# Throw-away matrix products on TensorE at a dozen of its waits in a two-block transformer kernel

## The reference, cut to what matters

```python
# first block, layer l
h = x * (1 + scale1) + shift1
y = token_mixer(h, ...)                       # attention branch + gated branch, then w_out
x = layer_norm(ALPHA * x + gate1 * y, ...)
y = moe_ffn(x * (1 + scale2) + shift2, ...)   # router, 64 experts, shared expert
x = layer_norm(ALPHA * x + gate2 * y, ...)
# second block
y, yc = attention_mixer(h, hc, ...)           # then MLP on x and on the context
y, _  = rwkv_mixer(h, hc, ...)                # wkv_scan forward and backward, group norm, read-out
x = x + gt2 * sq_relu_mlp(rmsnorm(x) * (1 + sc2) + sh2, w1, w2)
```

## Time and profile before

| | |
|---|---|
| median of 3 runs | 3715.33 us (3712.76 to 3722.76) |
| profiled execution, its own time | 3722.76 us |
| its span | 3722.7 us |
| TensorE busy | 3370.9 us, 91% |
| mean granted TensorE clock over the span | 0.956 |

### The profile page before, as it was taken

The page is one execution under the profiler, slowest core; times in us unless marked ns, Lnnn a source line. Parts: engine busy times, 40 slices in busy tenths (PEclk is TensorE's granted clock), DMA queues, the critical chain, the costliest instruction groups (busy, mean ns, idle before and its releaser), DMA issues.

```text
span 3722.7 us, 68873 instructions
## 1 busy us (share of the span) xinstructions
PE 3370.9 (91%) x29944; PEld 2469.4 (66%) x29944; DVE 1214.7 (33%) x2371; ACT 650.1 (17%) x1258; POOL 215.4 (6%) x186
## 2 busy tenths in 40 slices
PE   7998899999888889999979999999998889887899
PEld 5776466666667556656657664448877777786788
DVE  1344132233334323323345452010324454444200
ACT  0111011111110111111123231000023313332100
POOL 0000000000000000000000000000004410341000
PEclk9998999999899899999989999999999999998999
DMA  7655398899474469969912351224431013100342
GB/s 275 221 216 224 152 386 331 349 402 385 161 273 154 181 245 372 402 274 382 392 67 81 137 191 68 79 78 149 147 141 48 4 34 125 37 4 3 128 155 102
DMA packets 116171, 703.07 MB, mean 189 GB/s; under 512 B 11296, under 2 KB 11472, under 8 KB 49760
## 3 DMA queue, kind: packets, MB, share of 16 engines
q1 hardware_dynamic: 112224, 685.47, 47.5%
q0 software_dynamic: 3584, 12.25, 1.0%
HBM read 696.62 MB, written 1.05 MB: 187 GB/s over the span
## 4 chain that ended last, share of the span: by engine, by line
PE 41%; DVE 5%; ACT 2%; issue 1%; POOL 1%; DVEq 0%; ACTq 0%; POOLq 0%; PEldq 0%
PE ps L1518 9%; PE ps L1505 9%; PE ps L2148 7%; PE ps L204 4%; PE ps L1855 4%; DVE arena L137 2%; ACT arena L120 1%; PE ps L544 1%; PE ps L571 1%; PE ps L342 1%; PE ps L2530 1%; PE ps L2160 1%; PE ps L2153 1%; DVE arena L141 1%; PE ps L559 1%
## 5 line engine op out<-in xcount | busy, mean ns | idle before, releaser
L204 PE MATMUL ps<-arena 128*128 128x256 f32 (+2 forms) x2432 | 637.8, 425 | 45.6 <-issue 17.1
L204 PEld LDWEIGHTS ps<-arena 128*128 128x128 f32 (+1 forms) x2432 | 475.8, 197 | 201.6 <-issue 124.6
L120 ACT ACTIVATE arena<-ps 128x512 f32<-128x512 f32 (+1 forms) x526 | 265.2, 504 | 1632.6 <-PE ps L204 384.9
L1098 PE MATMUL ps<-arena 128*64 128x256 f32 x4096 | 484.9, 387 | 33.1 <-issue 32.9
L1098 PEld LDWEIGHTS ps<-arena 128*64 128x64 f32 x4096 | 320.3, 140 | 198.1 <-issue 91.6
L2148 PE MATMUL ps<-arena 64*64 64x64 f32 x10496 | 310.4, 226 | 53.6 <-issue 19.5
L1505 PE MATMUL ps<-arena 128*128 128x512 f32 (+1 forms) x1024 | 334.1, 489 | 10.3 <-DVE arena L146 10.3
L2148 PEld LDWEIGHTS ps<-arena 64*64 64x64 f32 x10496 | 296.9, 141 | 67.7 <-issue 34.5
L1518 PE MATMUL ps<-arena 128*128 128x256 f32 x1536 | 332.0, 379 | 0.0
L1518 PEld LDWEIGHTS ps<-arena 128*128 128x128 f32 x1536 | 291.8, 190 | 40.1 <-issue 0.5
L137 DVE TENSOR_TENSOR arena<-arena,ps 128x512 f32<-128x512 f32 (+1 forms) x276 | 163.1, 591 | 461.1 <-PE ps L2148 237.9
(11 more groups left out here) (190 smaller groups left out, 2557.8 us busy)
## 6 DMA issues: line engine op xcount, KB each, us to landing
arena<-in_w_gate SPq DMA_DIRECT2D x128, 1024.0 KB, 8.5
arena<-in_w_up SPq DMA_DIRECT2D x128, 1024.0 KB, 11.7
arena<-in_w_down SPq DMA_DIRECT2D x128, 1024.0 KB, 8.9
arena<-in_mlp SPq DMA_DIRECT2D x80, 1024.0 KB, 4.7
arena<-in_w_ada SPq DMA_DIRECT2D x48, 1024.0 KB, 7.2
arena<-in_ada SPq DMA_DIRECT2D x48, 1024.0 KB, 4.8
arena<-in_w_in SPq DMA_DIRECT2D x30, 1024.0 KB, 5.6
arena<-in_w_rkv SPq DMA_DIRECT2D x20, 1024.0 KB, 4.8
```

Of the source, the lines that this page charges most:

```text
L120: self.e.activation(out, in_, func, bias=bias, scale=scale, **more).then_inc(*self.done(key))
L204: ins = pe.matmul(out, a, b, start=start and i == 0, stop=stop and i == len(pairs) - 1)
L1098: ins = pe.matmul(psum.of["gu", l, new][64 * ab:64 * ab + 64, i_ * 256:i_ * 256 + 256], xe[:, k, new % 2 * 128 + 64 * ab:new % 2 * 128 + 6 ...
```

## The change

A helper `keep_warm(pe, b, n)` issues n fp32 products of the identity with 256 columns of `condr` into a bank that has been taken and freed; the real products overwrite the result. It is called at nine places of the source.

```diff
+        def keep_warm(pe, b, n):
+            for _ in range(n):
+                pe.matmul(b[:, 0:256], ident[:, :], condr[:, 0:256], start=True, stop=True)
@@ turned_pe, after the four banks are freed, before reach(ready(0))
+            keep_warm(pe, psum.of["turned", l, which, 0], (7 if which else 22) if l or which else 0)
@@ mixer_pe
-            reach(pe, *at["gated", l])
             for a in range(2):
                 b, old = psum.take(("obT", l, a), ("obT out", l, a))
                 freed(pe, old)
+                if a == 0:
+                    keep_warm(pe, b, 4)
+                    reach(pe, *at["gated", l])
@@ gather
                 freed(pe, old)
+                if Q == k == 0:
+                    keep_warm(pe, b, 7)
                 reach(pe, *at["chosen", l, Q])
@@ mlp_pe
+                    if i == c == 0:
+                        keep_warm(pe, b, (12, 6)[l])
@@ turning_pe(pe, s, src, warm=0)
+                if k2 == 0 and warm:
+                    keep_warm(pe, b, warm)
+                    reach(pe, *at["ln", ("moe", 1), 1])
@@ attention_pe
-            reach(pe, *at["ln", ("moe", 1), 1])
-            turning_pe(pe, 0, XS[:, :])
+            turning_pe(pe, 0, XS[:, :], 10)
@@ scan_pe, after the waits for ar, b and k
                     gb, old = psum.take(key("gb", q), key("gb out", q))
                     freed(pe, old)
+                    if q == 0 and d == 1 and j == 0:
+                        keep_warm(pe, gb, 8)
@@ rwkv_pe, read-out
+                    if i == c == 0:
+                        keep_warm(pe, b, 20)
```

More of the change, by code:

```diff
@@ L1616, in sums_of, with turning_pe @@
             return small[:, o:o + 4]
-        def turning_pe(pe, s, src):
+        def turning_pe(pe, s, src, warm=0):
             sv = src.rearrange("p (t n) -> p t n", t=2)
```

## The result

The changed kernel is slower. Its median is 3742.24 us (4 runs, 3736.79 to 3746.13) against 3719.05 us for the kernel before, run beside it (4 runs): a ratio of 1.0059, 95% interval 1.0045 to 1.0074, so 23 us more, where 7.8 us less were forecast (3707.5 us) and 3721 us was the upper end of the range. The profiled execution has a span of 3744.3 us, 21.6 more than the 3722.7 of before.

The account below looks back on a forecast made before the run. TensorE, busy 91% of the span with its clock dipping, was taken to bound the kernel. Gains of 22.5 us less 14.7 us of costs gave -7.8 us from 3715.33: 3707.5 us, range 3693 to 3721.

Parts of the forecast that it names:

- the price of a product: On TensorE, 0.427 us at the high clock, 0.85 at the low; 158 products, 67 us, no other queue moving.
- the term for the expert blocks: Seven blocks that run: half 1's transposes 0.77 us later each, 5.4 us lost; bounds 0 and 12.0.
- The one that ended slower: Leftover waits of 0.3 to 2.1 us still bring the clock down, gains go: 3731 us; chance 0.08.
- The gains at the warmed places: Products ahead of longer TensorE waits keep the clock high for the work behind: 22.5 us saved in all.
- attention: Products before the transposes, hidden by a 5.51 us wait for the normalised context; 2.3 us saved.
- read-out: 20 products ahead of a 10.59 us wait; 1.5 us saved, bounds 1.5 saved to 5.0 lost.
- first MLP: Products of 5.1 us hidden in a 6.42 us wait; 1.4 us saved on low-clock work.
- The 2.0 us added for chance: First MLP and read-out: 1.0 us more saved at each, as another execution has more work at the low clock.
- The turned tokens: Layer 1's mixer and two mixtures: clock falls all the same, 0.5 us saved each, 1.5 together; bounds 0 and 12.9.
- the rule on transposes: Skill page's claim that transposes don't count as TensorE busy; turned places would bring 0 instead of 1.5 us.
- The recurrences: Products behind the waits for `ar`, `b` and `k` delay the pairs: 6.8 us lost; bounds 0 and 13.7.
- The variance: Products at two sums that follow without a wait: 2.5 us lost net; bounds 0 and 6.8.

Follow-up runs that it names:

- block_unrun: Kernel before plus four products in only the 121 expert blocks that never run on these inputs; 3738.03 us, ratio 1.004.
- block_run: Kernel before plus four products in only the 7 expert blocks that run on these inputs; 3716.9 us, ratio 0.9986.
- no_block_scan_var: Changed kernel without the products in the expert blocks, in the recurrences and at the variance; 3694.17 us, ratio 0.9924 to the kernel before.
- waits_only: Changed kernel without expert-block and variance products, recurrence products moved ahead of their waits; 3690.4 us, ratio 0.9921 to the kernel before.
- waits_no_turned: waits_only without the 36 products at the three turned places; 3693.54 us, ratio 0.9923 to the kernel before.
- no_block: Changed kernel without the products in the expert blocks; 3705.63 us, ratio 0.9953 to the kernel before.

## Why the prediction was wrong

**The step that failed** is in the price of a product: "No other engine gets work, no DMA is added ... so no queue but TensorE's moves", and with it "158 products, 316 instructions" as the whole of what is added. That counts what is run. The diff adds code for 128 blocks, and the term for the expert blocks (5.4 us, bounds 0 to 12.0) was worked out for the 7 of them that run. The runs put the block at 37 us in the changed kernel, 34 of them waits with an instruction packet. About half of it (18 us in block_unrun) is there when not one product runs; the 7 blocks that run cost nothing that shows in the end (block_run), although in each the end of the transposes comes 0.8 to 0.9 us later, as forecast. The packets also say that "no DMA is added" was wrong: the instruction queue brings 301 in place of 291. With 37 in place of 5.4 the sum of the prediction would be +24 us; measured were +23. That they meet so well is in part luck, since three other terms were off by 2 to 6 us each, both ways. None of its rivals had this mechanism. The one that ended slower blamed waits left over at the warmed places; they kept their clock.

**The gains at the warmed places were right.** The prediction had 22.5 us for the places where a wait stands behind the products. no_block_scan_var has those alone. Its TensorE instructions matched one by one with those of before, the places bring 19.9 us: gated branch 2.9 twice (3.0 each forecast), gather 2.7 twice (3.1 and 3.0), attention 2.3 (2.3), second MLP 0.9 (1.7), read-out 1.5 (1.5), layer 0's first mixture 2.8 and layer 1's 1.0 (0.5 each), layer 1's mixer 0.2 (0.5), first MLP nothing (1.4). At the first MLP 0.8 us came and went again: the products there, now quicker, wait for VectorE at each next step (0.40 us at 2294.40). The attention's transposes came 4.3 us later and the work behind their wait still came earlier, as worked out. The 2.0 us added for chance, 1.0 each at the first MLP and the read-out, show at neither place.

By its medians no_block_scan_var gains more, 3722.3 - 3694.2 = 28 us, and its profiled span is 33.0 us shorter than that of before. Of these, 14.5 us are in the rounds of experts (1161.9 against 1176.4), where it runs no added product and its blocks have their old length; 6.3 us of that are fewer waits with an instruction packet (7.2 against 13.5). This part no term of the prediction had: it came by where the code lies or by chance, and not by a higher clock at the places.

**The turned tokens** behaved as forecast on the average: products and transposes ran at the high clock, and it fell right behind them. The stretches of the changed kernel behind both turned halves, for layer 1's mixer and its mixture:

```profile
957.00:966.00 9.00, 6.44 (x21) 5.28 (x22) 2.42 (x5) 3.54 (x5) 5.27 (x10) 0.62 0.72 163
...
1208.07:1218.31 10.24, 10.24 (x38) 9.25 (x38) 3.77 (x21) 1.94 (x3) 0.00 (x0) 0.50 1.00 404
```

The mixer's low stretch is not gone; it has moved 17 us, from 941.72 to 958.89. By the medians the sum by the rule on transposes (0 in place of 1.5 us) can't be told from mine. The traces of waits_only and waits_no_turned, matched in the same way, do tell: at the two mixtures and the mixer 2.8, 1.0 and 0.4 us come with the products, 0.5, 0.5 and 0.1 without, so the products bring 3.1 us, twice what was forecast and not nothing.

**The recurrences:** the place and the mechanism were right (waits unchanged, pairs later by the work itself), the size was not. 6.8 us took the high price for all 16; they ran mostly at the low one, 12.7 us of work, close to the upper bound of 13.7, of which some comes back in the pairs. Measured 8 to 12 us.

**The variance:** forecast 2.5 us, measured nothing that can be told.

Put together: -28 for the gains, +8 to +12 for the recurrences and +37 for the block make +17 to +21 us; the changed kernel is 23 us slower. Everything the prediction worked out from the timeline of instructions that run came within a few us, the recurrences the furthest off. What it did not count was the code that doesn't run.

## What to carry to other kernels

Price an edit inside a branch by how often the branch is not taken as well: code that is jumped over is still brought in, and here 4 products in 121 blocks that never ran cost 18 us and 12 cost 91. A gain of some 15 us in such rounds came here also with edits that touch nothing in the rounds; look where in the trace it arises before you credit it to the idea. In a profile the sign is idle time put down to the engine's own sequencer or to "issue" at the first line behind a branch, with nothing late, and an instruction queue whose packet count grows more than the count of instructions. Here throw-away products paid only ahead of a wait that is longer than they are, and where real work followed at once that asked for nothing more; behind the wait they cost their full time, at the low clock at that.

## What was not expected of the hardware

- A jump over a block can cost up to 4.4 us of standing still, with an instruction packet of 16 KB that starts inside it and the end 2.4 to 2.7 us behind that start. Even the kernel before has such waits in its rounds, 12 with 13.5 us; with 7 products less in each block not run there is none left, and it is 0.6% faster (0.9939 [0.9926, 0.9952]).
- The stall brings the clock down as well: behind the one at 579.48 it is 0.50 for 3.42 us, all of it work.
- 130 products, about 55 us at the price in the prediction, raised TensorE's busy time by 29.0 us only (3399.9 us in no_block, 3370.9 before), since other work ran quicker, and made the kernel faster, 0.9953.
